# A filler product in both places of every S5 half step, in a hybrid Hyena, GLA and S5 block

## The reference

```python
def step(x, u_blk):                       # S5, once per direction
    bu = einsum('btgi,gpi->btgp', u_blk, b_bar)
    _, xs = associative_scan(combine, (lam_bar, bu), axis=1)
    xs = xs + pows[None] * x[:, None]
    y = einsum('btgp,gip->btgi', xs, c_mat).real
...
m = (sigmoid(g_hy) * (y_hy @ w_hy) + sigmoid(g_gla) * (y_gla @ w_gla)
     + sigmoid(g_s5) * (y_s5 @ w_s5))
return m @ w_out
```

## Time and profile before

| what | us |
|---|---|
| median of 3 runs (lowest, highest) | 1395.66 (1392.37, 1396.29) |
| the profiled execution, its own time | 1396.8 |
| its span in the profile | 1394.6 |
| PE busy with products | 1200.0 (86% of the span) |
| PE busy with weight loads | 912.9 (65%) |
| DVE busy | 563.0 (40%) |
| ACT busy | 406.8 (29%) |
| POOL busy | 401.8 (29%) |

### The profile page before, as it was taken

One profiled execution on the slowest core, in us unless ns is written; L12 is line 12 of the kernel. 1 busy time (PEld: TensorE's weight loads), 2 busy tenths in 40 slices (PEclk: granted clock), 3 DMA queues, 4 the chain that ended last, 5 costly groups with the idle time before them and its releaser, 6 DMA issues.

```text
span 1394.6 us, 15262 instructions
## 1 busy us (share of the span) xinstructions
PE 1200.0 (86%) x5933; PEld 912.9 (65%) x5933; DVE 563.0 (40%) x998; ACT 406.8 (29%) x751; POOL 401.8 (29%) x339
## 2 busy tenths in 40 slices
PE   4699799787669788888498989989989999999996
PEld 1278658675357566666454457658878888888884
DVE  3764435643755677556308372323420001200013
ACT  2653214422343333242041110112433231233321
POOL 2033015402101113021031112303345555556541
PEclk9899889898878989888599999989999999999998
DMA  9711121932121022031150314264523323333211
GB/s 329 225 61 46 43 109 61 198 108 91 36 70 38 8 83 53 9 98 53 23 196 16 106 45 152 91 200 148 136 61 91 91 84 113 91 91 108 96 53 60
DMA packets 138291, 131.49 MB, mean 94 GB/s; under 512 B 13049, under 2 KB 125881, under 8 KB 137196
## 3 DMA queue, kind: packets, MB, share of 16 engines
q1 hardware_dynamic: 126432, 105.58, 26.3%
q0 software_dynamic: 3840, 15.40, 3.1%
q10 hardware_dynamic: 7948, 9.54, 2.3%
HBM read 119.49 MB, written 8.91 MB: 92 GB/s over the span
## 4 chain that ended last, share of the span: by engine, by line
PE 55%; DVE 14%; ACT 4%; issue 3%; DMA 1%; POOL 1%; ACTq 0%; DVEq 0%; POOLq 0%
PE psum L679 47%; PE psum L898 2%; PE psum L928 1%; PE psum L931 1%; PE psum L918 1%; PE psum L929 1%; DVE buf L1992 1%; POOL ring_lo L1219 1%; DVE buf L1971 1%; DVE buf L1969 1%; DMA buf<-in_w_out 1%; DVE buf L1970 1%; PE psum L908 0%; DVE hT_lo L2230 0%; DVE buf L1948 0%
## 5 line engine op out<-in xcount | busy, mean ns | idle before, releaser
L1219 POOL TENSOR_TENSOR ring_lo<-buf,ring_hi 128x512 fp32r<-128x512 f32 (+1 forms) x260 | 340.7, 1342 | 813.3 <-ACT ring_hi L1370 813.3
L679 PE MATMUL psum<-hT_hi,ring_hi 128*128 128x512 f32 x712 | 296.6, 417 | 10.7 <-POOL ring_lo L1219 5.3
L679 PE MATMUL psum<-hT_lo,ring_hi 128*128 128x512 f32 x712 | 285.2, 400 | 0.0
L679 PE MATMUL psum<-hT_hi,ring_lo 128*128 128x512 f32 x712 | 284.2, 399 | 0.0
L1370 ACT ACTIVATE ring_hi<-buf 128x512 fp32r<-128x512 f32 (+1 forms) x260 | 139.9, 611 | 234.0 <-PE psum L679 162.4
L679 PE MATMUL psum<-buf,buf 128*128 128x512 f32 (+1 forms) x448 | 192.0, 584 | 14.4 <-DVEq L1665 7.7
L679 PEld LDWEIGHTS psum<-hT_hi,ring_hi 128*128 128x128 f32 x712 | 139.7, 196 | 44.8 <-POOL ring_lo L1219 5.8
L679 PEld LDWEIGHTS psum<-hT_lo,ring_hi 128*128 128x128 f32 x712 | 139.3, 196 | 32.2 <-issue 3.9
L679 PEld LDWEIGHTS psum<-hT_hi,ring_lo 128*128 128x128 f32 x712 | 138.6, 195 | 30.2
L679 PEld LDWEIGHTS psum<-buf,buf 128*128 128x128 f32 x448 | 88.5, 199 | 104.3 <-issue 85.0
L2239 DVE TENSOR_TENSOR buf<-psum,buf 128x512 f32<-128x512 f32 x22 | 15.2, 692 | 222.1 <-PE psum L679 222.1
(11 more groups left out here) (328 smaller groups left out, 1784.1 us busy)
## 6 DMA issues: line engine op xcount, KB each, us to landing
buf<-in_w_in SPq DMA_DIRECT2D x26, 1024.0 KB, 5.3
buf<-in_w_mod SPq DMA_DIRECT2D x24, 1024.0 KB, 7.3
buf<-in_w_ffn_in SPq DMA_DIRECT2D x44, 512.0 KB, 5.1
buf<-in_w_ffn_out SPq DMA_DIRECT2D x8, 1024.0 KB, 5.1
scr_k<-buf POOLq DMA_DIRECT2D x4, 1024.0 KB, 5.5
buf<-scr_k POOLq DMA_DIRECT2D x4, 1024.0 KB, 8.2
buf<-in_w_out SPq DMA_DIRECT2D x4, 1024.0 KB, 5.6
buf<-in_w_ffn_out SPq DMA_DIRECT2D x4, 768.0 KB, 4.4
```

What stands on the lines that cost most here:

```text
L679: ins = nc.tensor.matmul(o, a, b, start=start and n == 0, stop=stop and n == len(pairs) - 1)
L1219: nc.gpsimd.tensor_tensor(ring_lo[:, a:a + n], ring[:, a:a + n], ring_hi[:, h + i * n:h + i * n + n].bitcast(fp32), SUB)\
```

## The change

The first filler place no longer asks which half it is in. Before, an odd half (n = 1) issued at A only what was left in `late`, and no unit.

```diff
         for m in range(2 * NB):
             b, n = divmod(m, 2)
             step("s5_r", b, n)
-            one_beside(n == 0)
+            one_beside()
             if m + 1 < 2 * NB:
                 step("s5_d", *divmod(m + 1, 2))
             step("s5_z", b, n)
...
             if m + 2 < 2 * NB:
                 step("s5_gen", *divmod(m + 2, 2))
             one_beside()
             step("s5_k", b, n)
```

## The result

The changed kernel takes 1416.66 us (median of 4 runs, 1415.82 to 1421.1) against 1395.97 for the kernel before in the same session (4 runs, 1392.37 to 1400.48). The ratio is 1.0149, with a 95% interval of 1.0117 to 1.0182: slower by 1.5%, about 20.7 us. The sign was forecast; the size was not: 1402 was named, and 1410 was the upper end of the range.

A forecast was written before the change was run, and what follows sets the result against it. The S5 stage was taken to bound the kernel as a chain between engines, none full. Terms 9.7 + 7.5 - 2.8 - 2.0 - 6.0 = +6.4 us on 1396.8 gave 1403.2, as median about 1402 us; range 1390 to 1410.

The forecast's parts named there:

- The sign: Whole kernel: the change was forecast to make it slower, with a chance of 0.59.
- 1, the late eviction ahead of K: Odd halves 1 to 9: the hy unit's eviction and a table load delay ACT's copy of K, so `s5_y`: +9.7 us.
- 2, `s5_y` at the slow clock: Halves 4 to 12: a new wait makes `s5_y` run slow, 5.4 us each in 4 to 10: +7.5 us, lower bound +1.9.
- the first two rivals: Filled waits (faster, 1387 us, chance 0.15) and a wash (1396.5 us, chance 0.22).
- 3, the unit at A: Odd halves 1 to 9: the added unit fills PE's wait for ACT, and `s5_z` starts sooner behind T: -2.8 us.
- 4, fast clock behind it: Odd halves 1 to 9: `s5_z` and B run at full clock, about 0.4 us each: -2.0 us.
- the rival of collisions: Halves 1, 5, 9: POOL's splits hold DVE and 1 MB loads may delay `Mt`: +14 us, 1410 us, chance 0.18.
- 5, the splits: Splits leave B, between `s5_gen` and ACT's copies; no size of its own, counted inside other terms' sums.
- 6, the bare end: Halves 10 to 15, with units gone from 11 on: shorter waits and a lost eviction, -6.0 us, bounds -3 to -8.
- the filled waits: Halves 1 to 9: ACT's copy of K is not held, `s5_y` starts 10.8 us behind T: -8.2, 1387 us, chance 0.15.
- the wash: Copy of K held as forecast, but `s5_y` runs half fast: sum +0.8, 1396.5 us, chance 0.22.

The follow-up runs named there:

- e2: Changed kernel with the hy unit's eviction in odd halves issued ahead of `s5_z`, gate units left late: 1402.05 us, ratio 1.0052 to the kernel before.
- e6: Changed kernel with the product of `s5_z` made seven times in even halves from 2 on, keeping PE busy before `s5_y`: 1409.35 us, ratio 1.0101.
- e5: Changed kernel, instruction order kept, PSUM banks of the unit at A and first `s5_d` product exchanged in halves 3, 5, 7, 9: 1404.78 us, ratio 1.0092.
- e3: Changed kernel with whatever the unit at A left issued ahead of `s5_z` in every half: 1371.72 us, ratio 0.9834 to the kernel before.
- e8: Kernel before, with what the unit at A left issued ahead of `s5_z` and splits ahead of `s5_k` moved behind `s5_w`: 1369.43 us, ratio 0.9804.

## Why the prediction came out wrong

**1, the late eviction ahead of K: right.** +10.6 for +9.7, with the copy of K, the table load and 12.6 us where they were put; e2 takes it away alone. What was left out is half a microsecond each in halves 1 and 7, where `s5_y` comes 7.0 us behind the end of the copy of K and not 6.6.

**2, `s5_y` at the slow clock: right in kind, a little small.** +6.0 for +7.5; half 10 was at the fast clock for part of it (3.78), though PE had waited 3.06 us there as in halves 4 and 6 (3.09 and 3.07). That the clock makes the length is shown by e6. In the lower bound there is a slip: four times 4.4 less 15.1 is 2.5, not 1.9. It puts the first two rivals 0.6 us too low and leaves the forecast as it is.

**3, the unit at A: the step that failed.** The prediction let the unit start when the transposes of `s5_w` end. That moment came out right (1.35 behind T), but the unit then waited 2.0 to 2.5 us for its PSUM bank in halves 3, 5, 7 and 9, 9.2 us in all, and in halves 3 and 7 ran at the slow clock for part of its length: +10.6 for -2.8. That miss of 13.4 us is most of the 16 us between forecast and measured length of the stage. The code had it to be seen: the job that the change adds is the eighth behind A of the even half, and there are eight banks. e5, by two bank numbers alone, takes 11.7 us out of this term (55.1 to 43.3). The sign of the forecast was no luck: with this wait gone, e5 is still slower than the kernel before, by 0.9% (0.6 to 1.3%), and its 1404.78 us is near the 1402 that was named for a kernel without it.

**4, fast clock behind it: too large.** -0.7 for -2.0. Halves 3 to 9 do take 7.2 us. Half 1 takes 8.9, since its split now falls on DVE's `s5_x` and `s5_v`, as the rival of collisions has it. Three instructions of it, of which the last two took 0.42 and 0.76 in the kernel before, and POOL's split (from timelines of DVE and POOL):

```profile
419.13 0.42 DVE L2025 TENSOR_TENSOR buf<-buf,psum 128x256 f32<-128x256 f32 x1 [3.03 <-PE psum L918]
419.66 1.28 DVE L2030 TENSOR_TENSOR buf<-buf,buf 128x256 f32<-128x256 f32 x1
421.04 1.66 DVE L1969 TENSOR_TENSOR buf<-buf,buf 128x576 f32<-128x576 f32 x1
```

```profile
416.89 5.19 POOL L1219 TENSOR_TENSOR ring_lo<-buf,ring_hi 128x512 fp32r<-128x512 f32 x4 [42.74 <-ACT ring_hi L1370]
```

L2030 and L1969 have both inputs in SBUF and ran 1.8 us longer in all; L2025, with one input in PSUM, took its usual 0.42 while POOL worked. The Trainium skill ("SBUF — State Buffer", § SBUF: two separate sides) says that a DVE instruction with two SBUF inputs is held by a POOL instruction that reads SBUF, and the rows agree. In halves 5 and 9 nothing is held, because the bank wait had moved `s5_z` past the split. In e3, without that wait, halves 1, 5 and 9 take 8.9 from `s5_z` to T for 7.5 in halves 3 and 7. Half of these 1.3 us is such a hold (L2032, 1.00 for 0.42); the other half is that ACT makes its four split copies ahead of the unit's eviction, so that `s5_x` starts 0.65 us later.

**5, the splits:** that they leave B was forecast, and no split stands in front of a copy of K in the changed kernel. That such a place matters is shown by e8 for the kernel before with early evictions, by 15.7 us; what it is worth in the changed kernel no run tests.

**6, the bare end: right in kind, too large.** -4.2 for -6.0. Halves 11 and 13 behave as written (8.82 and 8.83 to `s5_y`, forecast 8.9). Two terms were nothing. Half 11 did not gain (`s5_z` 9.55 behind T for 9.28), as `s5_d` ran slow in it. And the eviction of two DVE instructions, which stood in half 14 and not in 15, had been hidden behind PE's K product (L908) at the slow clock; from the end of the last but one `s5_y` to the start of the last it is 21.6 us in both kernels. Against them, half 13 had its `s5_z` 1.1 us sooner, which was in no term.

Of the rivals, the filled waits needed an unheld copy of K and did not come, and the wash needed `s5_y` half fast, which it was in half 10 alone. The collisions were real in one half only, and `Mt` was late by at most 0.5 us. The price of 1410 that this rival named was nearer to the truth than the forecast, but that was luck, as the cause was another.

## What to carry to other kernels

Before work is put into a wait, count which buffer it opens: in a ring of eight banks, one more job between two others changes who waits for whom, and the new job waits for the eviction of the job eight back, however late that stands in its engine's queue. What is done with a filler's result matters more than the filler: here its place in ACT's and DVE's queues decided some 45 us, and the second product itself nothing that could be measured. And where waits alternated with work on PE, a wait could cost twice, once as itself and once by the clock of what followed; a gain at one wait can be handed to the next, as in e2 and e6.

## What the hardware showed beyond what was expected

Behind waits of 2.0 and 2.2 us the unit at A ran at the fast clock (5.6 and 5.5 us to `s5_d`, halves 5 and 9). Behind waits of 2.5 (halves 3 and 7) it began fast, was slow from 1.4 to 4.3 us after its start, and was fast again (7.2 us). Behind waits of 3.3 to 3.6 in e6 it was slow from its first product. The wait alone does not decide: behind 3.06 us `s5_y` of half 10 began fast, and behind 0.94 us `s5_y` of half 12, where `s5_d` ahead of it had run slow too, was slow throughout (5.35 us). Two edits that gave 24.3 and 14.6 us gave 45 together; with waits of 0.8 to 1.3 us left ahead of `s5_y` in e3, all of its products in halves 2 to 10 took 2.9 us.
